# Modulation of a two-layer decoder trunk on TensorE: blocks of ada_w as weights, one column of c as the moving operand

## What is computed

```python
c_act = jax.nn.silu(c)                                   # (1, 1024)
for l in range(DEPTH):
    mod = c_act @ ada_w[l] + ada_b[l]                    # ada_w[l]: (1024, 6144)
    sh_m, sc_m, g_m, sh_f, sc_f, g_f = jnp.split(mod, 6, axis=-1)
    h = _rmsnorm(x, norm_mix_g[l]) * (1.0 + sc_m[:, None]) + sh_m[:, None]
    cols = h @ w_in[l]
    ...                                                  # three kinds of mixing heads
    x = x + g_m[:, None] * mix
    h = _rmsnorm(x, norm_ffn_g[l]) * (1.0 + sc_f[:, None]) + sh_f[:, None]
    x = x + g_f[:, None] * peer_ffn(h, peer_wq[l], peer_subkeys[l], peer_u[l], peer_v[l])
return _rmsnorm(x, final_norm_g)
```

## Time and profile before

| | us |
|---|---|
| time, median of 3 runs | 1839.49 (1839.48 to 1844.95) |
| the profiled execution, its own time | 1839.77 |
| its span, first to last instruction | 1837.9 |
| VectorE busy | 1398.9 (76%) |
| TensorE busy | 1314.2 (72%), weight loads 769.6 |
| end of the lead: first dot product of the expert part starts | 285.01 |

### The profile page before, as it was taken

How to read it: one execution, slowest core, us unless ns; L and a number is a source line. 1 busy time by engine, 2 the same in 40 slices (tenths; PEclk the granted TensorE clock), 3 DMA queues, 4 the chain that set the end, 5 groups by cost and what they waited for, 6 DMA issues and landing times.

```text
span 1837.9 us, 26377 instructions
## 1 busy us (share of the span) xinstructions
PE 1314.2 (72%) x9588; PEld 769.6 (42%) x9588; DVE 1398.9 (76%) x3327; ACT 663.5 (36%) x1634; POOL 517.6 (28%) x564
## 2 busy tenths in 40 slices
PE   2768787787877866787877867787877865555554
PEld 2657675453544534453444534443544531111111
DVE  5878588999974747999965748999965769985554
ACT  2313114444832233445732135336732233231112
POOL 2110012232332222232323232232422233343331
PEclk9875688897998987898988978898988977777777
DMA  9993669998999998999999999998999999999996
GB/s 393 421 396 139 229 240 403 401 415 352 361 420 421 421 420 355 383 414 367 400 421 421 420 420 372 393 422 339 378 421 421 421 421 420 404 405 421 421 421 261
DMA packets 97010, 706.42 MB, mean 384 GB/s; under 512 B 10992, under 2 KB 11504, under 8 KB 13296
## 3 DMA queue, kind: packets, MB, share of 16 engines
q0 software_dynamic: 80640, 587.24, 78.6%
q1 hardware_dynamic: 16240, 117.50, 15.7%
HBM read 703.64 MB, written 1.05 MB: 383 GB/s over the span
## 4 chain that ended last, share of the span: by engine, by line
DVE 43%; DMA 28%; PE 18%; issue 6%; ACT 4%; POOL 0%; DVEq 0%; ACTq 0%; POOLq 0%
DMA ringmem<-in_peer_uv_dram,eidx 23%; DVE ringmem L1451 15%; PE psum L785 5%; DMA W<-in_w_groups_dram 3%; PE psum L661 3%; PE psum L420 2%; DMA ringmem<-in_ada_pairs_dram 2%; DVE coef L1464 2%; DVE ringmem L1095 1%; PE psum L648 1%; DVE cand L1166 1%; DVE cand L1168 1%; DVE eid L1169 1%; DVE attn L1237 1%; DVE ast L1238 1%
## 5 line engine op out<-in xcount | busy, mean ns | idle before, releaser
L785 PE MATMUL psum<-ringmem,diag 64*64 64x512 f32 x4096 | 612.6, 724 | 280.8 <-ACT diag L1066 280.5
L387 POOL DMA_INDIRECT ringmem<-in_peer_uv_dram,eidx x512 | 492.0, 961 | 1082.3 <-PE psum L785 967.6
L1451 DVE SCALAR_TENSOR_TENSOR ringmem<-ringmem,psum 128x1024 f32<-128x1024 f32 x512 | 613.1, 1219 | 240.7 <-DMA ringmem<-in_peer_uv_dram,eidx 227.4
L785 PEld LDWEIGHTS psum<-ringmem,diag 64*64 64x64 f32 x4096 | 151.8, 154 | 605.8 <-ACT diag L1066 399.9
L1066 ACT ACTIVATE diag<-K,coef 128x128 f32<-128x128 f32 x512 | 176.5, 393 | 259.3 <-DVE coef L1464 258.9
L1058 ACT ACTIVATE coef<-dots 128x2 f32<-128x2 f32 x256 | 52.0, 203 | 509.9 <-DVE ringmem L1451 509.2
L420 PE MATMUL psum<-hT,W 128*128 128x128 f32 x1344 | 183.8, 298 | 40.4 <-DMA W<-in_w_groups_dram 22.1
L420 PEld LDWEIGHTS psum<-hT,W 128*128 128x128 f32 x1344 | 172.8, 210 | 83.5 <-issue 39.3
L1095 DVE SCALAR_TENSOR_TENSOR ringmem<-ringmem,diag 128x1024 f32<-128x1024 f32 x96 | 115.5, 1223 | 23.6 <-DMA ringmem<-in_ada_pairs_dram 21.4
L661 PE MATMUL psum<-hT,W 128*128 128x128 f32 x1024 | 126.1, 280 | 7.1 <-ACT hT L835 7.1
L661 PEld LDWEIGHTS psum<-hT,W 128*128 128x128 f32 x1024 | 120.1, 195 | 22.3 <-issue 12.2
(11 more groups left out here) (243 smaller groups left out, 1599.9 us busy)
## 6 DMA issues: line engine op xcount, KB each, us to landing
ringmem<-in_ada_pairs_dram POOLq DMA_DIRECT2D x48, 1024.0 KB, 18.4
W<-in_w_pieces_dram SPq DMA_DIRECT2D x48, 1024.0 KB, 9.4
W<-in_w_groups_dram SPq DMA_DIRECT2D x24, 1536.0 KB, 11.6
W<-in_w_groups_dram SPq DMA_DIRECT2D x12, 1024.0 KB, 9.7
ringmem<-in_peer_uv_dram,eidx POOLq DMA_INDIRECT x512, 14.9
W<-in_w_groups_dram SPq DMA_DIRECT2D x4, 1040.0 KB, 9.2
attn<-in_subkeys_t_dram SPq DMA_DIRECT2D x4, 1024.0 KB, 9.4
K<-in_consts_dram SPq DMA_DIRECT2D x1, 1546.0 KB, 18.3
```

What stands on the lines that cost most here:

```text
L387: nc.gpsimd.indirect_dma_start(slot(k), None, rows, bass.IndirectOffsetOnAxis(ap=eidx[:, ph % 2, m:m + 1], axis=0)).then_inc(row_landed[q ...
L785: mm = nc.tensor.matmul(acc_part(r, half), diag[d, k % DIAGS, d], slot(k)[d, D + half * 512:D + (half + 1) * 512], start=(k % SEL == 0), s ...
L1451: ins = v.scalar_tensor_tensor(out=u, in0=u, scalar=1.0, in1=hrep, op0=ALU.mult, op1=ALU.mult, accum_out=dots[:, j:j + 1])
```

## The change

The modulation moves from VectorE to TensorE.

- The host lays ada_w out by rows: a slot is now 128 rows of ada_w (one block of the contraction) by 2048 output columns, two sections of a layer. There are six groups (ADA_GROUPS, three pairs of sections for each of two layers) of eight slots. The number of slots, their size, the ring and the gathers after them stay.
- c comes in as a column layout, 128 by 8 (`ccol`), and silu is taken of that.
- TensorE's `ada(q)` waits for slot q and issues 16 matmuls: each has a block of 128 by 128 of the slot as its weights and one column of `ccol` as its moving operand, and adds into one column of a PSUM bank (bank 0 or 1, by the group's parity). The last of them frees the slot. TensorE's lead has the 48 slots between its segments by the new table, `LEAD`: three before segment 1, five before segment 2, then one in two segments up to 28 (13 slots), and 0.9 for each segment after that (27 slots, the last behind segment 58).
- VectorE has no chunks left. Once for each group, `modulation(g)` waits for the group's last slot, adds ada_b from PSUM into `MC`, and forms the scale where the group holds one. ScalarE waits for group 2 at segment 57.
- SyncE's first weights for the projections wait for the landing of slot 6, where they waited for slot 5.

```diff
@@ -66,10 +66,9 @@
 SUBG, LAM, LAMC, BF, PSMALL = 0, HD, HD + 128, HD + 130, HD + 134
 
 
-SECTIONS = (1, 0, 2, 4, 3, 5)
 SH_M, SC_M, G_M, SH_F, SC_F, G_F = range(6)
-ADA_CHUNKS = DEPTH * 6 * KD
-ADA_SLOTS = ADA_CHUNKS // 2
+ADA_GROUPS = DEPTH * 3
+ADA_SLOTS = ADA_GROUPS * KD
 
 
 UNITS = [("d", h) for h in range(DIFF_H)] + [("f", h) for h in range(FOX_H)]
@@ -110,11 +109,11 @@
 def lead_pace():
 
 
-    due, out = 2.0 * KD, [1] * (2 * KD - 1) + [2]
+    due, out = 1.0 * KD, [0] * 3 + [1] * (KD - 3)
     for seg in range(2, SEGMENTS):
-        due += 1.3 if seg <= 28 else 1.0 if seg <= 56 else 1.5
-        out += [seg] * (int(min(due, ADA_CHUNKS)) - len(out))
-    return out + [SEGMENTS] * (ADA_CHUNKS - len(out))
+        due += 0.5 if seg <= 28 else 0.9
+        out += [seg] * (int(min(due, ADA_SLOTS)) - len(out))
+    return out
 
 
 
...
@@ -272,7 +271,7 @@
         subg, lamc, bfb = prow[:, SUBG:SUBG + HD], prow[:, LAMC:LAMC + 2], prow[:, BF:BF + FOX_H]
         lamp = prow[:, LAM:LAM + 128].rearrange("p (a b) -> p a b", a=4)
         BTK, KTK, ATK, VTK = range(4)
-        crow = diag[:].rearrange("p a c -> p (a c)")
+        ccol = diag[:, 0, 0:KD]
         gdiag = (hT[:, 0:4, :], hm[:, 0:512].rearrange("p (a c) -> p a c", a=4))
 
         def acc_part(r, half):
@@ -310,11 +309,11 @@
 
             @block.sync
             def _(sp):
-                sp.dma_start(crow, c.broadcast_to([P, D])).then_inc(s["c_in"], 16)
+                sp.dma_start(ccol, c).then_inc(s["c_in"], 16)
                 sp.dma_start(pcols[:], param_cols.rearrange("l p n -> p l n")).then_inc(s["pcol_in"], 16)
                 sp.dma_start(xs[:], x.rearrange("o (t p) d -> p (o t) d", p=P)).then_inc(s["x_in"], 16)
                 sp.dma_start(K[:], consts).then_inc(s["const_in"], 16)
-                sp.wait_ge(row_landed[5], 16)
+                sp.wait_ge(row_landed[6], 16)
 
                 def mixing(i):
                     l = i // NT
@@ -375,7 +374,7 @@
                     elif q >= 3:
 
                         pool.wait_ge(row_landed[q - 3], 16)
-                    nc.gpsimd.dma_start(ringmem[:, q % RING, :], ada_pairs[q:q + 1].rearrange("o p d -> (o p) d")
+                    nc.gpsimd.dma_start(ringmem[:, q % RING, :], ada_rows[q:q + 1].rearrange("o p d -> (o p) d")
                                         ).then_inc(row_landed[q % RING], 16)
                 rows = peer_uv.rearrange("a e d -> (a e) d")
                 for k in range(PHASES * SEL):
@@ -787,7 +786,27 @@
                                                   start=(k % SEL == 0), stop=(k % SEL == SEL - 1), skip_group_check=True)
                         mm.then_inc(freed(k)[0], 1)
 
-                Pace(mixing(0)).upto(END - 1)
+                def ada(q):
+
+
+                    g, k = divmod(q, KD)
+                    if k == 0 and g >= 2:
+                        pe.wait_ge(s["mod_ready"], g - 1)
+                    if q == 0:
+                        pe.wait_ge(s["c_ready"], 1)
+                    pe.wait_ge(row_landed[q % RING], 16 * (q // RING + 1))
+                    for b in range(2 * KD):
+                        mm = nc.tensor.matmul(bank[g % 2][:, b:b + 1], ringmem[:, q % RING, b * P:(b + 1) * P],
+                                              ccol[:, k:k + 1], start=(k == 0 and b == 0), stop=(k == KD - 1),
+                                              skip_group_check=True)
+                    mm.then_inc(slot_free[q % RING], 1)
+
+                lead = Pace(mixing(0))
+                for q in range(ADA_SLOTS):
+                    lead.upto(LEAD[q])
+                    ada(q)
+                lead.upto(END - 1)
+                pe.wait_ge(s["mod_ready"], ADA_GROUPS)
                 place_h(0)
                 for ph in range(PHASES):
                     beside = Pace(mixing(ph + 1) if ph + 1 < PHASES else last_gate())
@@ -908,7 +927,7 @@
                         if seg == 1:
                             scaled(1)
                         elif seg == 2:
-                            act.wait_ge(s["mod_ready"], 1 if l == 0 else 3)
+                            act.wait_ge(s["mod_ready"], 1 if l == 0 else ADA_GROUPS)
                             modulated(1, SH_M, SC_M)
                         elif seg == 6:
                             act.wait_ge(s["mixed_x"], at("mixed_x", i, 1))
@@ -1007,6 +1026,8 @@
                         elif seg == 56:
                             scaled(2)
                         elif seg == 57:
+                            if i == 0:
+                                act.wait_ge(s["mod_ready"], 3)
                             modulated(5, SH_F, SC_F)
                         n = seg - QRY0 - 3
                         if 0 <= n < 2 * PH and n % 2 == 0:
@@ -1068,7 +1089,7 @@
 
                 act.wait_ge(s["c_in"], 16)
                 act.wait_ge(s["eps_set"], 2)
-                nc.scalar.activation(crow, crow, ACT.Silu).then_inc(s["c_ready"], 1)
+                nc.scalar.activation(ccol, ccol, ACT.Silu).then_inc(s["c_ready"], 1)
                 Pace(mixing(0)).upto(END - 1)
                 for ph in range(PHASES):
                     beside = Pace(mixing(ph + 1) if ph + 1 < PHASES else ending())
@@ -1086,33 +1107,21 @@
                 v = nc.vector
                 step = Steps(dve, "dve_step")
 
-                def ada(j):
-
-                    q, a = divmod(j, 2)
-                    l, r = divmod(j, 6 * KD)
-                    dve.wait_ge(row_landed[q % RING], 16 * (q // RING + 1))
-                    u = ringmem[:, q % RING, a * D:(a + 1) * D]
-                    ins = v.scalar_tensor_tensor(out=u, in0=u, scalar=1.0, in1=crow, op0=ALU.mult, op1=ALU.mult,
-                                                 accum_out=MC[:, l, SECTIONS[r // KD], r % KD:r % KD + 1])
-                    if a:
-                        step.count[q % RING] = step.count.get(q % RING, 0) + 1
-                        ins.then_inc(slot_free[q % RING], 1)
-                        dve.wait_ge(slot_free[q % RING], step.count[q % RING])
-
-                def modulation(l, first, end, last):
-
-                    b = pcols[:, l, ADAB + first * KD:ADAB + end * KD]
-                    part = MC[:, l, first:end, :].rearrange("p a k -> p (a k)")
-                    step(v.tensor_tensor(part, part, b, ALU.add))
-                    for section, gain in ((SC_M, GMIX), (SC_F, GFFN)):
-                        if first <= section < end:
-                            a = MC[:, l, section, :]
-                            ins = v.scalar_tensor_tensor(out=a, in0=a, scalar=1.0, in1=pcols[:, l, gain:gain + KD],
-                                                         op0=ALU.add, op1=ALU.mult)
-                            if last and (section == SC_F or end <= SC_F):
-                                step(ins, "mod_ready")
-                            else:
-                                step(ins)
+                def modulation(g):
+
+                    l, a = g // 3, 2 * (g % 3)
+                    dve.wait_ge(slot_free[(KD * g + KD - 1) % RING], (KD * g + KD - 1) // RING + 1)
+                    if g == 0:
+                        dve.wait_ge(s["pcol_in"], 16)
+                    b = pcols[:, l, ADAB + a * KD:ADAB + (a + 2) * KD]
+                    part = MC[:, l, a:a + 2, :].rearrange("p a k -> p (a k)")
+                    scale, gain = ((SC_M, GMIX), (None, None), (SC_F, GFFN))[g % 3]
+                    told = () if scale else ("mod_ready",)
+                    step(v.tensor_tensor(part, bank[g % 2][:, 0:2 * KD], b, ALU.add), *told)
+                    if scale:
+                        m = MC[:, l, scale, :]
+                        step(v.scalar_tensor_tensor(out=m, in0=m, scalar=1.0, in1=pcols[:, l, gain:gain + KD],
+                                                    op0=ALU.add, op1=ALU.mult), "mod_ready")
 
                 def rstd(name, value):
                     dve.wait_ge(s[name], value)
@@ -1483,22 +1492,10 @@
                 step(v.memset(stat[:, 4:5], RMS_EPS), "eps_set")
                 step(v.memset(stat[:, 5:6], LN_EPS), "eps_set")
                 lead = Pace(mixing(0))
-                lead.upto(0)
-                dve.wait_ge(s["c_ready"], 1)
-                for j in range(ADA_CHUNKS):
-                    ada(j)
-                    if j == 4:
-                        lead.upto(1)
-                    if j == 2 * KD - 1:
-                        dve.wait_ge(s["pcol_in"], 16)
-                        modulation(0, SH_M, G_M, True)
-                    elif j == 6 * KD - 1:
-                        modulation(0, G_M, 6, True)
-                    elif j == ADA_CHUNKS - 1:
-                        modulation(1, SH_M, G_M, False)
-                        modulation(1, G_M, 6, True)
-                    if j >= 2 * KD - 1:
-                        lead.upto(LEAD[j])
+                for q in range(ADA_SLOTS):
+                    lead.upto(LEAD[q])
+                    if q % KD == KD - 1:
```

(8 more changed lines are left out.)

4 lines of the change are left out of this document (2 added, 2 removed).

## The result

The kernel after takes 2078.74 us (median of 4 runs, 2069.64 to 2085.28) against 1839.89 us for the kernel before: a ratio of 1.129, 95% interval 1.124 to 1.133. The profiled execution took 2074.53 us, 4.2 us under that median, with a span of 2072.7; the forecast was 2055, in a range of 1980 to 2140.

What follows compares the result with a forecast made beforehand. The lead was taken as bound by DMA up to 123 us, then TensorE. Its stretches, 70 + 131 + 259 + 41.5 = 501.5 us instead of 285.0 (+216.5), gave 2055 us, range 1980 to 2140.

Steps and rivals of the forecast that it cites:

- Start to segment 2: Start of the lead: eight cold slots 54.4 us, transposes 3.3, first slot there at 9.42; 70 us, where before 37.65.
- Segments 2 to 28: Projection stretch of the lead: TensorE's own 63.5 us plus 13 slots at 5.2 each; 131 us.
- Half and half: Slots alternating with runs of 16 projection matmuls: priced at the mean of full and half clock, 5.2 us each.
- Segments 28 to 57: Later lead: TensorE's own work 97 us plus 27 slots, three quarters cold, at 6.0 each; 259 us.
- Segment 57 to the end: End of the lead: 41.5 us as before, nothing gained from VectorE's 28 chunks less.
- Expert part: After the lead: no instruction of it changes, so 0 us.
- the clock column: Sign in the profile after: granted clock of 0.5 to 0.6 before the first projection.
- the DMA share in the lead: Sign in the profile after: DMA share over the lead well under a half.
- cold throughout: Rival, lead: clock never rises before segment 57; 2164 us; mostly cold (2110 to 2170) given 0.18.
- Warm throughout: Rival, lead: load stream holds 2.4 GHz; 1892 to 1926 us; mostly or all warm (1890 to 2000) given 0.18.
- Faster: Rival, slots: one-column records overlap; decides at 1.3 us a slot, 0.04 a record; faster by over 0.3% given 0.03.
- It doesn't do what it says: Rival, lead: slots wait for other engines' segments and delay segment 46's gate or the second norm; adds nothing; no separate chance.

Runs made afterwards that it cites:

- few: Kernel after with one matmul (16 moving columns) per slot in place of 16, leaving out 15 of 16 modulation columns: 1849.74 us, ratio 1.0039 to the kernel before.
- wide128: Kernel after with each of the 768 slot matmuls moving 128 columns, c and 127 of zeros, in place of one: 1922.65 us.
- all_first: Kernel after with all 48 slots placed ahead of segment 2: 2122.55 us.
- both: Kernel before, VectorE's chunks kept, plus the 48 slots' matmuls on TensorE at the kernel after's places, on constants with unused results: 2070.07 us.

## Why the prediction was right, and where its terms were off

The mechanism was right: the loss is TensorE's own added time in its own queue, at a mixed clock, and nothing is gained on VectorE. That the total came within 1.2% owes something to luck, since errors cancel in two of the stretches. The forecast was 2056 against the profiled execution's 1839.77; the profiled one after took 2074.5. Its steps, by the stretches:

- **Start to segment 2: 70 us forecast, 66.4 measured.** Eight slots took 54.7 us (forecast 54.4). The transposes stayed at 1.95 us and not 3.3: the 1.97 us of the earlier trace rows were already at half clock (granted 0.50 from 240 to 242 us), so there was nothing to scale. The first slot was ready at 7.97 instead of 9.42.
- **Segments 2 to 28: 131 forecast, 128.2 measured,** but from two errors that cancel. The slots took 4.01 us each, not 5.2, 52 us in place of 67; TensorE's own part took 128.3 - 52.1 = 76 us, not 63.5. I had charged the lower clock to the slots; most of it fell on the projections behind them. Half and half was right for the two together and wrong for each.
- **Segments 28 to 57: 259 forecast, 259.1 measured,** which is luck to this degree. The forecast counted 27 slots at 6.0, of which two stand behind the cut: it was 25 slots, 155.6 us or 6.2 each, nearly all cold, and 103 us for the rest instead of 97, some 10 of them idle (waits of the chain that I had granted away in full: TensorE was busy 249.0 of 259.0).
- **Segment 57 to the end: 41.5 forecast, 63.6 measured.** This is the term that was mis-sized, by 22 us, more than the whole miss of 18.5. 13.9 us are the two slots which I had counted a stretch too early; 3.6 us are the standstill beside the gathers, which I hadn't seen coming since nothing in the trace of before shows it; the other 4 to 5 us fit the query products, which keep TensorE busy for 37.8 us in place of 32.1, at a granted 0.50 where they stand between the last slots. The prediction also took 28 chunks off VectorE here; in this stretch there were 16 (28 is the number of the stretch before), which changes nothing in its sum.
- **Expert part: 0 forecast, +2.5 us measured** in the profiled execution. I can't place it; it is inside the spread of the kernel after (2069.64 to 2085.28).

What the removal is worth: I granted TensorE all of its idle time, 52 us, as filled. few, with the chunks gone, still has 43 us of it, so VectorE's chunks had caused little; it vanished because slots were put into it, as the sum had it.

Of the signs that the prediction named, two came out otherwise: the clock column shows 1.00 and not 0.5 to 0.6 before the first projection (the pitch there is that of half clock, see the last section), and the DMA share in the lead is 0.47, hardly "well under a half".

The rivals: **cold throughout** failed between segments 2 and 28 (mean clock 0.77, not 0.5), though it holds for the first stretch, and nearly so from 28 to 57 (0.56). **Warm throughout** was priced at 1892 to 1926 us, and wide128, which is the same kernel with its clock kept up, took 1922.65: the price was right and the condition false. By the Trainium skill (TensorE: Matmul & The Clock Gate, Part 1) the gate is set by how busy TensorE has been; all_first, with 307 us of one-column loads without a gap, all at the half-clock pitch, speaks against that sentence as it stands. By the same page of the Trainium skill, section LDWEIGHTS, a load of 128 columns takes 107 ns, with no clock named; for float32 the runs show a pitch of 0.112 us at full clock, which agrees, and of 0.213 us at half clock, which doesn't. **Faster** fell with its condition: the records start every 0.112 us at best, where 0.04 was needed. **It doesn't do what it says** fell too: both, whose slots wait for nothing but the constants, takes at most 6 us less from segment 2 to 57.

## What to carry to other kernels

A product with one vector is bound by its weight loads on TensorE: at a given clock 128 by 128 float32 weights cost the same whether 1 or 128 columns stream past. So putting it there can pay only if TensorE has that much idle time at that place and the work removed elsewhere was being waited for. Price such an insertion twice, at full and at half clock, and ask what it does to the clock of its neighbours; if the loads must be paid anyway, widening the moving operand with zeros can be a gain. And an engine's busy time that is removed is worth only what waited for it: without its 117 us of chunks (few) the kernel was no faster at all.

## What the runs showed of the hardware that was not expected

- 128 times the moving columns made the program 156 us faster (2078.7 to 1922.7 us), at the same pitch of 0.112 us at full clock and with a granted clock of 0.98 in place of 0.56 from segment 28 to 57.
- The lower clock can fall on the neighbour: slots between projections ran at a pitch of 0.112 us at a granted 1.00 (71.6 to 75.0 us), and the projections behind took 5.45 us for 32 records instead of 3.73, at a granted 0.67 (75.1 to 80.3 us).
- Before the first recorded change the clock column is not to be trusted: it shows 1.00 for 8 to 66.3 us of the kernel after, where the slots' pitch is 54.7 us / 256 = 0.214, that of half clock. The eight transposes there took 1.95 us, as they did at a granted 0.50 in the kernel before; eight products of the same shape at a granted 1.00 took 1.04 us (516.23 us in the kernel after).
- With the first expert gathers issued beside the queries, TensorE stood still between two heads for 3.6 to 6.5 us in five kernels; with the gathers held back, in the one kernel where this was tried, it didn't. The path is open.
